# The first sparse tile's down rows summed by TensorE on four column groups, dense queries and ups in three passes

## The chip, the cores and the metric

One core of a Trainium2 chip. The metric is device time in microseconds of one execution: 2183.6 us before, the median of 3 runs (2182.3 to 2185.1).

## The reference

One layer over T = 640 tokens (512 of a prompt, 128 of eight streams), d = 1024: gated conv and retention branches, then a PEER layer, then a norm. The change touches PEER alone:

```python
q = (hb @ w_q)                       # 8 heads x 2 sides x 128
s = einsum(q, sub_keys)              # scores of 128 keys a side
# top 16 a side, top 16 of their sums: 16 experts e a head, weights g = softmax
a = gelu(einsum('thkd,td->thk', u_tab[e], hb))   # "ups": dot with row e of u
out = einsum('thk,thkd->td', g * a, v_tab[e])    # "downs": weighted sum of rows of v
```

There are 128 x 128 experts, and each token uses 128 of them. All is float32.

## The kernel before

Five tiles of 128 tokens. The first NS = 2 are **sparse**: for each of 256 "rows" r (a tile and one of its 128 picks), GpSimd gathers one row of u and one of v for each of the 128 tokens (128 x 1024, 512 KB each, one token in a partition). VectorE takes the dot with h (`dot`, L1446), ScalarE the gelu and the weight (`pair_gelu`), and VectorE adds weight times the v row to x (`pair_step`, L1463). Rows come in pairs, a pair's dots run two pairs ahead. The other three tiles (TD = 384 tokens) are **dense**: every up tile e of 128 experts is multiplied with h of all 384 tokens (`up`, L1833), gelu by ScalarE on the way out of PSUM (L950), stored to `acts` in DRAM; the gates (softmax weights, zero where an expert isn't picked) are built from one-hots by VectorE (`onehots`, L1483 and L1485: 48 blocks of 8 tokens) and TensorE (`scatter`, L1848), and stored as `gates`. Then 128 down tiles: VectorE forms p = acts x gates (`weigh`, L1500) and TensorE adds p times the v tile (`down_three`, L1890 to L1892).

A product in "three passes" splits both float32 operands into a high part (ScalarE's copy to F32R) and a low part (VectorE's difference) and sums high x high, high x low, low x high in single-pass F32R matmuls. Before, w_in, w_out and the downs (lows L1509 and L1515, highs L996 and L998) work so; queries (L1793) and ups are plain f32 matmuls.

Order: sparse queries (2 x 16 tiles of wq), dense queries (16 tiles), ups (128), downs (128). SP loads each tile of 512 KB to a ring of four (`plain_in`, L623) once the tile four before it has been used. VectorE runs retrieval (top 16, L1354 to L1428) for the five tiles, with pairs between its steps; then the 48 one-hot blocks with eight pairs; six pairs before the downs and 48 beside them (`pair_at`, `pair_after`). TensorE's scores and turns stand at fixed up tiles (SCORES_AT, PICKT_AT). GpSimd's gathers go through 14 slots in a fixed order (`rows_order`, L732), each waiting for the slot's last user.

## Time and profile before

| | |
|---|---|
| median of 3 runs | 2183.6 us |
| the profiled execution | 2185.9 us, its span 2184.1 |
| TensorE matmul busy | 98% of the span |
| VectorE / ScalarE / GpSimd busy | 80% / 28% / 39% |
| DMA | 732 MB, mean 335 GB/s |

A busy share counts an engine's instructions and not what the end waits for; the chain of waits goes back from the last instruction to what released it. In a list of single instructions the distance from start to start is the pace; the duration shown can overlap the next one's. An f32 matmul shows as two records, an F32R matmul as one.

### The profile page before, as it was taken

The page shows a single profiled execution, that of the slowest core. Times are in us where ns is not written, and L with a number is a line of the kernel's source. Part 1 is how long each engine was busy: PE and PEld are TensorE (multiplying, and loading weights), DVE is VectorE, ACT ScalarE, POOL GpSimd, SP SyncE. Part 2 cuts the span into 40 slices and gives each one's busy share as a digit, 9 for nine tenths or more (in the row PEclk, how much of TensorE's full clock was granted, in tenths as well). Part 3 has the DMA queues.
Part 4 walks back from the last instruction along what each step waited for, and adds up shares of the span by engine and source line. Part 5 has one row for each costly group of instructions (what it writes and reads, how often), then busy time and mean ns, then how long its engine had stood idle before and what let it go on. Part 6 is the DMA issues. An engine that isn't in the chain of part 4 may idle for free.

```text
span 2184.1 us, 31103 instructions
## 1 busy us (share of the span) xinstructions
PE 2139.8 (98%) x10569; PEld 1706.0 (78%) x10569; DVE 1746.6 (80%) x3270; ACT 619.3 (28%) x1197; POOL 860.8 (39%) x606
## 2 busy tenths in 40 slices
PE   6999999999999999999999999999999999999997
PEld 6999989999998985655565565677767888888886
DVE  2577586676765286898989979999969999999998
ACT  4212213132223111121211211233324444443434
POOL 4222122223333004475685675411145444444440
PEclk9999999999999999999999999999999999999999
DMA  5999999989983458999999999888999999999995
GB/s 191 300 329 308 300 299 330 333 299 326 305 287 136 137 195 336 336 372 412 397 410 412 383 412 412 299 290 298 301 340 411 414 414 413 414 414 414 414 415 202
DMA packets 312713, 732.28 MB, mean 335 GB/s; under 512 B 30208, under 2 KB 162048, under 8 KB 312576
## 3 DMA queue, kind: packets, MB, share of 16 engines
q1 hardware_dynamic: 188352, 436.52, 55.4%
q0 software_dynamic: 73728, 268.47, 31.3%
q10 hardware_dynamic: 50496, 25.59, 3.9%
q8 instruction: 70, 1.15, 0.2%
q14 instruction: 67, 0.55, 0.1%
HBM read 602.46 MB, written 128.00 MB: 334 GB/s over the span
## 4 chain that ended last, share of the span: by engine, by line
PE 61%; DMA 16%; DVE 14%; issue 4%; SPq 2%; ACT 1%; POOL 0%; DVEq 0%; ACTq 0%
PE ps L1833 29%; DMA b<-acts 12%; PE ps L1793 6%; PE ps L1596 6%; PE ps L1595 6%; PE ps L1594 6%; DMA b<-in_u_t 4%; PE ps L1848 4%; DVE b L1463 3%; DVE b L1509 2%; DVE b L1446 1%; DVE b L1515 1%; DVE b L1500 1%; SPq L527 1%; DVE b L1103 1%
## 5 line engine op out<-in xcount | busy, mean ns | idle before, releaser
L1833 PE MATMUL ps<-b,b 128*128 128x384 f32 x2048 | 665.6, 486 | 0.0
L732 POOL DMA_INDIRECT b<-u_rows,b x256 | 362.6, 1416 | 677.9 <-DVE b L1446 489.1
L1833 PEld LDWEIGHTS ps<-b,b 128*128 128x128 f32 x2048 | 386.8, 190 | 263.4
L695 POOL TENSOR_TENSOR b<-b,b 128x1024 fp32r<-128x1024 f32 x80 | 196.8, 2463 | 468.6 <-ACT b L745 464.0
L1463 DVE SCALAR_TENSOR_TENSOR b<-b,b,b 128x1024 f32<-128x1024 f32 x256 | 330.8, 1292 | 49.0 <-ACT b L966 32.6
L1594 PE MATMUL ps<-b,b 128*128 128x320 f32 x1152 | 364.5, 316 | 0.0
L1595 PE MATMUL ps<-b,b 128*128 128x320 f32 x1152 | 357.0, 310 | 0.0
L1596 PE MATMUL ps<-b,b 128*128 128x320 f32 x1152 | 357.0, 310 | 0.0
L732 POOL DMA_INDIRECT b<-in_peer_v,b x256 | 288.8, 1128 | 118.1 <-issue 76.9
L1446 DVE CUSTOM_DVE_ANT_0 b<-b,b 128x1024 f32<-128x1024 f32 x256 | 312.5, 1221 | 25.3 <-DMA b<-u_rows,b 23.8
L1103 DVE STREAM_TRANSPOSE b<-b 128x1024 f32<-128x1024 f32 x128 | 158.0, 1241 | 186.5 <-DMA b<-in_u_t 178.7
L1890 PE MATMUL ps<-b,b 128*128 128x512 f32 x768 | 299.5, 390 | 2.9 <-DVE b L1515 2.9
L1891 PE MATMUL ps<-b,b 128*128 128x512 f32 x768 | 299.9, 391 | 0.0
L1892 PE MATMUL ps<-b,b 128*128 128x512 f32 x768 | 298.7, 389 | 0.0
L1594 PEld LDWEIGHTS ps<-b,b 128*128 128x128 f32 x1152 | 217.6, 189 | 1.0
L1595 PEld LDWEIGHTS ps<-b,b 128*128 128x128 f32 x1152 | 217.4, 189 | 1.0
L1596 PEld LDWEIGHTS ps<-b,b 128*128 128x128 f32 x1152 | 217.2, 189 | 0.0
L950 ACT ACTIVATE b<-ps 128x384 f32<-128x384 f32 x128 | 62.6, 489 | 494.2 <-PE ps L1833 494.2
L1890 PEld LDWEIGHTS ps<-b,b 128*128 128x128 f32 x768 | 144.0, 188 | 35.9 <-issue 4.8
L1891 PEld LDWEIGHTS ps<-b,b 128*128 128x128 f32 x768 | 144.2, 188 | 30.1
L1892 PEld LDWEIGHTS ps<-b,b 128*128 128x128 f32 x768 | 144.2, 188 | 30.0
L1509 DVE TENSOR_TENSOR b<-b,b 128x1024 fp32r<-128x1024 f32 x128 | 155.8, 1217 | 12.3 <-ACT b L996 9.7
(164 smaller groups left out, 2414.0 us busy)
## 6 DMA issues: line engine op xcount, KB each, us to landing
b<-in_u_t SPq DMA_DIRECT2D x256, 512.0 KB, 6.5
u_rows<-b SPq DMA_DIRECT2D x512, 128.0 KB, 4.4
b<-in_peer_v SPq DMA_DIRECT2D x128, 512.0 KB, 22.1
b<-in_w_in SPq DMA_DIRECT2D x72, 512.0 KB, 6.4
b<-in_wq SPq DMA_DIRECT2D x48, 512.0 KB, 4.4
gates<-b ACTq DMA_DIRECT2D x12, 2048.0 KB, 8.3
b<-gates SPq DMA_DIRECT2D x32, 768.0 KB, 17.4
acts<-b SPq DMA_DIRECT2D x120, 192.0 KB, 7.9
```

The lines of the kernel that those rows point to most:

```text
L695: nc.gpsimd.tensor_tensor(lo[u][:, :], raw[:, u, :], hi[u][:, :].bitcast(F32), ALU.subtract).then_inc(lo_ready, 1)
L732: nc.gpsimd.indirect_dma_start(slots[n % SLOTS][:, :], None, u_rows if kind == "u" else v_rows, bass.IndirectOffsetOnAxis(ap=row_id[:, r_ ...
L1446: nc.vector.tensor_tensor_reduce(up_row, up_row, h_row[:, r_ // P, :], 1.0, 0.0, ALU.mult, ALU.add, dots[:, r_ // PAIR % LINES, r_ % PAIR: ...
L1463: nc.vector.scalar_tensor_tensor(token_rows, down_row, row_w[:, b % LINES, i:i + 1], token_rows, ALU.mult, ALU.add).then_inc(row_done, 1)
L1509: nc.vector.tensor_tensor(v_lo[n % HALVES][:, :], down_tile(e), v_hi[n % HALVES][:, :].bitcast(F32), ALU.subtract).then_inc(v_split, 1)
L1594: nc.tensor.matmul(out, wa_hi[u][:, cols], h_hi[:, k, tok], start=(k == 0), stop=False)
L1595: nc.tensor.matmul(out, wa_hi[u][:, cols], h_lo[:, k, tok], start=False, stop=False)
L1596: last = nc.tensor.matmul(out, wa_lo[u][:, cols], h_hi[:, k, tok], start=False, stop=(k == KT - 1))
L1833: last = nc.tensor.matmul(ps[:, up_bank(e), 0:TD], w[:, k * P:(k + 1) * P], h2[:, k, SD:T], start=(k == 0), stop=(k == KT - 1))
L1890: nc.tensor.matmul(out, p_hi[:, u, tok], v_hi[n][:, cols], start=(e == 0), stop=False)
L1891: nc.tensor.matmul(out, p_hi[:, u, tok], v_lo[n][:, cols], start=False, stop=False)
L1892: last = nc.tensor.matmul(out, p_lo[:, u, tok], v_hi[n][:, cols], start=False, stop=(e == NKEY - 1))
```

## The change

- `NPAIR` counts the second sparse tile's pairs only: 64, with 6 beside the one-hots, 4 before the downs (`NPAIR_U` = 10) and 54 beside the downs.
- First sparse tile: all 128 dots first (5 in each of the 9 gaps of the second retrieval, the others behind it). One gelu and one multiplication give all weights. Row numbers and weights are turned by TensorE, and GpSimd gathers the down rows per token ("t": the 128 v rows of one token, one in a partition), in the order of four quarters of 32 tokens. In each of 32 steps (`sum_rows`, behind one up tile each, m = 77 to 108) TensorE sums four tokens' rows: 4 tokens x 2 halves of 512 columns, f32, each with 32 columns of weights (a window that is zero but for the token's own column), to its quarter of the PSUM partitions. VectorE adds the result to x once.
- Dense queries and ups (N3 = 144 tiles, m = 0 to 143) in three passes: ScalarE makes the tile's high part (`up_tile_high`), VectorE the low part in place of the raw tile (`lows`), TensorE 24 F32R matmuls (`in_three`). The three high buffers lie in the memory of the sparse tokens' h.
- Where VectorE makes the lows, and where the one-hots' scatters, scores and turns stand on TensorE, is computed by a planner (`plan`).
- x of the dense tiles is stored to DRAM (`x_kept`) before the queries and read back in the downs, since the high part of dense h takes its memory. One v tile, not two, is loaded ahead of the downs.

```diff
-NPAIR = ROWS // PAIR
+NPAIR = P // PAIR
+N3 = 2 * PH + NKEY
+HIGHS = 3
+WINDOWS = 4
+SUM_GROUPS = 4
+NSUM = P // SUM_GROUPS
+DOTS_AT_FIRST = 4
+DOTS_INSIDE = 5
+DOTS_BEHIND_HOT = 7
+PAIRS_BESIDE_HOTS = 6
+BEFORE_DOWNS = 4
+LEAD = 3.0
...
+    def retrieval(tt, inside=()):
+        for i in range(INSIDE + 1):
+            yield ("retrieval", tt, i), 5.2
+            if 0 < i:
+                for step in inside:
+                    yield step()
+            if i in (2, 6):
+                yield ("inside", tt, i), 0.0
+        yield ("retrieved", tt), 0.0
+    dots = iter(range(P))
+    yield from retrieval(0)
+    for _ in range(DOTS_AT_FIRST):
+        yield ("dot", next(dots)), 1.25
+    yield from retrieval(1, [lambda: (("dot", next(dots)), 1.25)] * DOTS_INSIDE)
+    for r_ in dots:
+        yield ("dot", r_), 1.35
+    yield ("dots_done",), 3.0
+    for tt in range(NS, TT):
+        yield from retrieval(tt)
+    b = 0
+    yield ("picks_out",), 6.0
+    for blk_ in range(NHOT):
+        yield ("hot", blk_), 3.25
+        if blk_ == DOTS_BEHIND_HOT:
+            for r_ in range(AHEAD * PAIR):
+                yield ("dot", P + r_), 1.25
+        for _ in range(pairs_behind_hot(blk_)):
+            yield ("pair", b), 5.0
+            b += 1
+    for _ in range(BEFORE_DOWNS):
+        yield ("pair", b), 5.0
+        b += 1
+    yield ("end",), 0.0
...
+    lows, begins = {}, [812.0]
+    t, n, sums_at, hots_at = 772.0, 0, N3, N3
+    hots_end = 2 * PH + FIRST_DOWN
+    def hot_tile(blk_):
+        return hots_at + blk_ * (hots_end - hots_at) // NHOT
+    def begin(m):
+        while len(begins) <= m:
+            i = len(begins) - 1
+            us = 4.25 if i < 2 * PH else 4.4
+            if sums_at <= i < sums_at + NSUM:
+                us += 2.0
+            if hots_at <= i < hots_end:
+                us += 1.8 * sum(1 for b in range(NHOT) if hot_tile(b) == i)
+            begins.append(begins[-1] + us)
+        return begins[m]
+    for key, us in dve_steps():
+        if key == ("hot", 0):
+            hots_at = n + 1
+        if key[0] == "hot" and key[1] >= HOTS:
+            t = max(t, begin(hot_tile(key[1] - HOTS) + 1))
+        if key == ("dot", P):
+            t = max(t, begin(sums_at + NSUM) + 1.0)
+        while n < N3 and (begin(n) - LEAD <= t or key == ("end",)):
+            n += 1
+            t += 1.15
+        if key == ("retrieval", NS, 1):
+            sums_at = n + 1
+        lows[key] = n
+        t += us
+    return lows, sums_at, [hot_tile(b) - 2 * PH for b in range(NHOT)]
...
+def token_of(q):
+    return (q % SUM_GROUPS) * (P // SUM_GROUPS) + q // SUM_GROUPS
 def rows_order():
-    order = [("u", r) for r in range(AHEAD * PAIR)]
-    for r in range(ROWS):
+    order = [("u", r) for r in range(P)]
+    order += [("t", q) for q in range(P)]
+    order += [("u", P + r) for r in range(AHEAD * PAIR)]
+    for r in range(P, ROWS):
...
+        raw_lo = at(x_from + TT * D * 4, [P, GROUP, D], F32R)
+        u_hi = [at(o_, [P, D], F32R) for o_ in (h_from + 36864, h_from, h_from + 4096)]
...
+                if i == 2 * GROUP - 1:
+                    for tt in range(NS, TT):
+                        sp.wait_ge(xs_ready, TT + tt + 1)
+                        sp.dma_start(x_kept[tt - NS, :, :], x[:, tt, :]).then_inc(x_stored, 16)
...
+            for i in range(ND):
+                sp.dma_start(x[:, NS + i, :], x_kept[i, :, :]).then_inc(x_back[i], 16)
...
+                if (kind, r_) == ("t", 0):
+                    pool.wait_ge(idT_ready, 1)
...
+            def dense_high(i):
+                if i == 0:
+                    act.wait_ge(x_stored, 16 * ND)
+                tok = slice(i * P, (i + 1) * P)
+                act.wait_ge(h_ready, 2 * TT + 2 * (NS + i) + 2)
+                nc.scalar.activation(hd_hi[:, :, tok], h2d[:, :, tok], ACT.Copy).then_inc(hd_high, 1)
+            def up_tile_high(m):
+                i = 2 * A_WQ + m
+                act.wait_ge(loaded[i % GROUP], 16 * ((N_WQ + i) // GROUP + 1))
+                act.wait_ge(a_used, A_MIX + (2 * A_WQ if m < HIGHS else i - HIGHS + 1))
+                nc.scalar.activation(u_hi[m % HIGHS][:, :], raw[:, i % GROUP, :], ACT.Copy).then_inc(up_high, 1)
...
+            def window(j):
+                if j == 0:
+                    act.wait_ge(wT_ready, 1)
+                    act.wait_ge(zeros_ready, 1)
+                if j >= WINDOWS:
+                    act.wait_ge(rows_summed, j - WINDOWS + 1)
+                src = wT_a[:, :].rearrange("p (c j) -> p c j", c=SUM_GROUPS)[:, :, j:j + 1]
+                nc.scalar.activation(windows[:, j % WINDOWS, :, 31:32], src, ACT.Copy).then_inc(window_ready, 1)
...
+            def lows(*key):
+                while low_next[0] < LOWS[key]:
+                    m = low_next[0]
+                    at_ = (2 * A_WQ + m) % GROUP
+                    dve.wait_ge(up_high, m + 1)
+                    nc.vector.tensor_tensor(raw_lo[:, at_, :], raw[:, at_, :], u_hi[m % HIGHS][:, :].bitcast(F32),
+                                            ALU.subtract).then_inc(up_low, 1)
+                    low_next[0] += 1
+            def dense_low(i):
+                tok = slice(i * P, (i + 1) * P)
+                dve.wait_ge(hd_high, i + 1)
+                nc.vector.tensor_tensor(hd_lo[:, :, tok], h2d[:, :, tok], hd_hi[:, :, tok].bitcast(F32),
+                                        ALU.subtract).then_inc(hd_ready, 1)
...
-            retrieval(0)
-            for r_ in range(AHEAD * PAIR):
-                dot(r_)
-            for tt in range(1, TT):
-                retrieval(tt, next_pair)
-                for i in range(GAP if tt < TT - 1 else 0):
-                    next_pair()
-                    if i == 1 and tt >= NS:
-                        picks_out(tt)
-            assert taken[0] == NPAIR_R
...
+                def between():
+                    seen[0] += 1
+                    lows("retrieval", tt, seen[0])
+                    if tt == 1:
+                        if seen[0] == 2:
+                            row_numbers_out()
+                        for _ in range(DOTS_INSIDE):
+                            next_dot()
+                    if tt == NS and seen[0] == 1:
+                        row_weights_out()
+                    if tt == TT - 1 and seen[0] >= 8:
+                        picks_out(seen[0] - 8 + NS)
+                return between
...
+            lows("retrieval", 0, 0)
+            retrieval(0, inside(0))
+            lows("retrieved", 0)
+            for _ in range(DOTS_AT_FIRST):
+                next_dot()
+            lows("retrieval", 1, 0)
+            retrieval(1, inside(1))
+            lows("retrieved", 1)
+            while at_dot[0] < P:
+                next_dot()
+            lows("dots_done")
+            row_weights()
+            for tt in range(NS, TT):
+                lows("retrieval", tt, 0)
+                retrieval(tt, inside(tt))
+                lows("retrieved", tt)
+            lows("picks_out")
             picks_out(TT - 1)
-            for blk_ in range(TD // BLK):
+            for blk_ in range(NHOT):
+                lows("hot", blk_)
+                if HOT_AT[blk_] == UP_IN_TWO - 4 and HOT_AT[blk_ - 1] < UP_IN_TWO - 4:
+                    row_sums_out()
                 onehots(blk_)
-                if blk_ % 6 == 4:
+                if blk_ == DOTS_BEHIND_HOT:
+                    for r_ in range(P, P + AHEAD * PAIR):
+                        lows("dot", r_)
+                        dot(r_)
+                for _ in range(pairs_behind_hot(blk_)):
                     next_pair()
             for i in range(BEFORE_DOWNS):
-                if i == WEIGH_BEFORE:
-                    down_inputs(0)
                 next_pair()
+            lows("end")
...
+            def in_three(m, out):
+                pe.wait_ge(up_low, m + 1)
+                hi, lo = u_hi[m % HIGHS][:, :], raw_lo[:, (2 * A_WQ + m) % GROUP, :]
+                for k in range(KT):
+                    cols = slice(k * P, (k + 1) * P)
+                    nc.tensor.matmul(out, hi[:, cols], hd_hi[:, k, :], start=(k == 0), stop=False)
+                    nc.tensor.matmul(out, hi[:, cols], hd_lo[:, k, :], start=False, stop=False)
+                    last = nc.tensor.matmul(out, lo[:, cols], hd_hi[:, k, :], start=False, stop=(k == KT - 1))
+                last.then_inc(a_used, 1)
+            def dense_query(m):
+                i = 2 * A_WQ + m
+                pe.wait_ge(evac, A_MIX + i - 1)
+                in_three(m, ps[:, 2 + i % UP_BANKS, 0:TD])
...
+            def sum_rows(j):
+                pe.wait_ge(window_ready, j + 1)
+                places = [PLACE["t", j * SUM_GROUPS + c] for c in range(SUM_GROUPS)]
+                for n in places:
+                    pe.wait_ge(row_in[n % SLOTS], 16 * (n // SLOTS + 1))
+                for dh in range(2):
+                    for c, n in enumerate(places):
+                        last = nc.tensor.matmul(ps[32 * c:32 * c + 32, 2 + dh, :],
+                                                windows[:, j % WINDOWS, c, 31 - j:63 - j],
+                                                slots[n % SLOTS][:, dh * 512:(dh + 1) * 512],
+                                                start=(j == 0), stop=(j == NSUM - 1))
+                last.then_inc(rows_summed, 1)
...
+            for m in range(N3):
+                if m < A_WQ:
+                    dense_query(m)
+                else:
+                    up(m - A_WQ)
...
+                if 0 <= m - SUMS_AT < NSUM:
+                    sum_rows(m - SUMS_AT)
+                for blk_ in range(NHOT):
+                    if HOT_AT[blk_] == m - A_WQ:
```

## Rows read from the trace of the kernel before

**Rows 1.** The page's 40 slices: TensorE's clock, and what DMA moved.

```profile
PEclk9999999999999999999999999999999999999999
...
GB/s 191 300 329 308 300 299 330 333 299 326 305 287 136 137 195 336 336 372 412 397 410 412 383 412 412 299 290 298 301 340 411 414 414 413 414 414 414 414 415 202
```

**Rows 2.** Stretches: us, busy PE PEld DVE ACT POOL, PEclk, DMA share, GB/s.

```profile
886.00:1392.00 506.00, 506.00 (x1637) 302.66 (x1636) 462.71 (x1107) 95.11 (x294) 321.99 (x250) 1.00 1.01 394
...
1392.00:1604.00 212.00, 211.12 (x1157) 159.25 (x1156) 203.52 (x496) 73.43 (x150) 39.99 (x35) 1.00 0.88 289
...
1646.00:2155.00 509.00, 507.59 (x2232) 418.37 (x2231) 483.50 (x656) 215.02 (x396) 233.20 (x178) 1.00 1.01 408
```

**Rows 3.** The chain of work, pieces merged: start, us, what.

```profile
797.89 7.21 PE ps L1793 x32
...
1268.98 123.84 PE ps L1833 x384
...
1600.80 3.57 PE ps L1848 x32
...
1604.37 36.14 PE ps L1833 x112
...
1831.21 20.82 DMA b<-acts
```

**Rows 4.** The down matmuls of L1890: durations, first and last start.

```profile
L1890 PE MATMUL ps<-b,b x768: 387/389/689, 1645.2 to 2172.6; 128*128 128x512 f32 x192
```

**Rows 5.** TensorE in order of time: w_in products, downs.

```profile
559.70 0.31 PE L1595 MATMUL ps<-b,b 128*128 128x320 f32 x1
...
569.53 0.31 PE L1596 MATMUL ps<-b,b 128*128 128x320 f32 x1
...
1789.70 0.39 PE L1892 MATMUL ps<-b,b 128*128 128x512 f32 x1
...
1801.98 0.39 PE L1892 MATMUL ps<-b,b 128*128 128x512 f32 x1
```

**Rows 6.** VectorE in order of time: the first retrieval, the first dot.

```profile
769.52 0.30 DVE L1354 MAX8 b<-ps 128x8 f32<-128x128 f32 x1 [24.13 <-PE ps L1819]
...
817.07 0.29 DVE L1428 SCALAR_TENSOR_TENSOR b<-b 128x128 uint32<-128x128 f32 x1
...
822.39 1.23 DVE L1446 CUSTOM_DVE_ANT_0 b<-b,b 128x1024 f32<-128x1024 f32 x1 [5.03 <-DMA b<-u_rows,b]
```

**Rows 7.** Groups by line: operands, count, busy us, mean ns, idle before.

```profile
L1833 PE MATMUL ps<-b,b 128*128 128x384 f32 x2048 | 665.6, 486 | 0.0
...
L996 ACT ACTIVATE b<-b 128x1024 fp32r<-128x1024 f32 x128 | 134.1, 1048 | 14.9 <-PE ps L1892 14.9
```

**Rows 8.** VectorE in the downs: a low, a pair, the next tile.

```profile
1657.78 1.21 DVE L1509 TENSOR_TENSOR b<-b,b 128x1024 fp32r<-128x1024 f32 x1
...
1658.92 0.54 DVE L1515 TENSOR_TENSOR b<-b,b 128x384 fp32r<-128x384 f32 x1
...
1663.69 1.22 DVE L1446 CUSTOM_DVE_ANT_0 b<-b,b 128x1024 f32<-128x1024 f32 x1
...
1668.41 0.55 DVE L1500 TENSOR_TENSOR b<-b,b 128x384 f32<-128x384 f32 x1
```

**Rows 9.** VectorE: the first of two one-hot blocks.

```profile
1394.38 2.14 DVE L1483 TENSOR_SCALAR b<-b,b,b 128x128 f32<-128x128 f32 x8
...
1397.69 2.13 DVE L1483 TENSOR_SCALAR b<-b,b,b 128x128 f32<-128x128 f32 x8
```

**Rows 10.** DMA in 1646 to 2155 us: total; acts loads, median us to landing.

```profile
DMA packets 52709, 207.88 MB, mean 408 GB/s; under 512 B 5873, under 2 KB 5873, under 8 KB 52675
...
b<-acts SPq DMA_DIRECT2D x30, 768.0 KB, 20.1
```

**Rows 11.** Loads of up tiles (L623), 1101 to 1388 us.

```profile
DMA to landing us min/median/max: 5.1/6.7/8.5
```

**Rows 12.** VectorE's waits in 1646 to 2155 us: us, times, longest.

```profile
DVE b L1500 <- DMA b<-acts: 22.9, 12, 2.6
```

321 lines of the change are left out of this document (203 added, 118 removed).

## Prediction

> **What bounds the kernel now.** I read the slices of the page first, then busy time by stage, then the chain of work, then single instructions. The slices [rows 1] say that TensorE is busy nearly throughout, at full clock, and that the DMA engines move 412 to 415 GB/s in many slices, which is the most they reach anywhere. The table by stage [rows 2] shows two stages behind 810 us. From 810 to 1646 us (dense queries, ups, scatters) TensorE has no idle time, VectorE is 91 to 96% busy beside the ups and the scatters, and DMA is near its top. From 1646 to 2155 us (downs) three things are close together: TensorE without a gap, VectorE 483.5 of 509 us, DMA 408 GB/s. The chain [rows 3] walks along TensorE alone in the first: 24 up tiles in 123.84 us, so **5.16 us a tile**, a scatter of two blocks 3.57, so **1.785 us** a block (and 3.57 for the scores of a tile, which are as many matmuls of the same shape), ups over at 1640.5. The first down matmul is at 1645.2 [rows 4]. In the downs the chain goes through VectorE's rows and the acts load (20.8 us), so it is no longer plainly TensorE: whatever loads VectorE or DMA more will lengthen it.
>
> **Dense queries and ups in three passes.** An up tile is now 8 f32 matmuls, recorded as 16 of 0.3225 us; the change makes them 24 of one pass. Their price is read where the kernel already does this: 320 columns, 67 steps from 559.70 to 569.53, 0.1467 us each; 512 columns, 54 steps in 12.28 us, 0.2274 [rows 5]. Over columns/2.4 GHz that is 13.4 and 14.1 ns, so 384 columns take 0.174 us, a tile 4.17, with hand-over **4.2 us**; bounds 4.16 and 4.32 (w_out's 512-column pitch of 0.233 adds 20 ns). The gain is 144 x 0.96 = 138 us.
>
> Its start is later: the high parts lie in the memory of the sparse tokens' h, so they wait for the last sparse query. That one ends at 797.89 + 7.21 - 5.16 = 799.9 [rows 3]. The lows of tiles 0 and 1 stand in VectorE's order before the last tenth of the first retrieval, which runs 769.5 to 817.4 (47.9 us [rows 6]), at about 809.5. So the first dense tile starts at **811** instead of 799.9: 11 us lost.
>
> The added halves: 144 highs on ScalarE at 1.05 us [rows 7], which is 28% busy, so nothing. 144 lows on VectorE at **1.15 us** of its time (the same low in the downs: 1657.78 to the next start at 1658.92 [rows 8]), 166 us. The queries' three dense halves (3 x 1.2 us) and the stores of x_kept fall into VectorE's wait of 24 us before 769.5 [rows 6]; the three ScalarE copies that feed them stand before the sparse queries' evacuations and may hold TensorE back by 2 us there, if two PSUM banks don't cover 3.2 us. On SP the stores of x_kept stand before sparse query tile 8's load; what they wait for (the scaled rows) is done by then, so nothing. If that cover failed, the tile loads behind it would come late by as much.
>
> **The first sparse tile's down rows.** 128 adds leave VectorE. But 140 leave this stage, as only 20 of the second tile's rows are now done before the downs instead of 160 rows of both; and 152 dots instead of 164. At 1.20 and 1.15 us a row ([rows 8]: a pair with dots is 1663.69 to 1668.41, 4.72 us) that is -168 - 14 + 166 = **-16 us** for VectorE before the downs. TensorE gets 32 steps of 8 matmuls, 16 records of 512 columns, 0.3225 x 512/384 = 0.43 us each. No row has column groups. Bounds: all four groups side by side, 4 x 0.43 = 1.7 us a step; none, 16 x 0.43 = 6.9. I take **2.2**, near the lower end, because the four groups write disjoint quarters of the partitions and in the nearest rows [rows 5] a matmul follows the last at 14 ns over its columns, so its weights load beside running work.
>
> The Trainium skill ("TensorE: Matmul & The Clock Gate", part 3) has three column tiles of 32 at 2.38 times the speed of one after another; carried to four that would be an estimate of 2.2 us, and no run here shows it yet.
>
> **The stage as a sum.** TensorE from 811: 144 x 4.2 = 604.8; scores of four tiles 4 x 3.57 = 14.3; turns 3; sums 32 x 2.2 = 70.4; scatters 48 x 1.785 = 85.7; together 778, so 1589. VectorE from 769.5: five retrievals 239.5; 132 dots x 1.26 = 166; lows 166; 48 one-hot blocks x 3.31 [rows 9] = 159; ten pairs 47; gathers' first landing 7 [rows 6]; small steps 8: together 792, so 1562. Both fit, but they are tied: each low stands at a fixed place of VectorE's order and its tile can't start before it. So phase by phase, with the places that the planner's arithmetic gives (74 lows before the dots end, 105 before the picks, 136 before the sixth pair, 144 at the end). POOL, which issues the gathers, now waits once for the turned row numbers before the down rows; behind it nothing but those rows is queued, and they come ready near 860, long before dot 128. ScalarE's new waits (a window for the sums, three steps ahead) stand before evacuations that have two banks of cover. Up to tile 74: TensorE 311 + 7 = 318 (1129), VectorE 769.5 + 96 + 161 + 85 + 8 = 1119; TensorE leads. Tiles 74 to 105: TensorE 206 (1335), VectorE 144 + 36; TensorE. One-hots: VectorE 159 + 5 + 28 + 35 = **227**, TensorE 218; VectorE leads, begin 1332, so 1562 with some stalls. Last eight tiles 34: **1596**. With the same 4.7 us to the first down it stands at **1600**, 45 us earlier than 1645.2.
>
> DMA in this stage: from 823 (row numbers) to 1119 the dots' 128 rows, 74 tiles and 58 stored acts are 67 + 39 + 11 = 117 MB, 283 us at 0.414 MB/us: it fits barely. In the sums each step wants 4 x 0.524 + 0.721 = 2.82 MB, 6.8 us against 6.4, made up by 14 rows fetched ahead: no cost taken, 10 us as the bound.
>
> **The downs.** 108 adds and 104 dots are left instead of 96 and 92, six pairs more: 6 x 4.72 = 28 us of VectorE. Bytes: 24 rows x 0.524 + 1.57 (x read back) = 14.1 MB on 207.9 [rows 10]; 222/0.4145 = 536 us for what took 509, +27. VectorE: 483.5 + 28.3 + its waits of 25.5 = 537, +28. Two resources are then full together, which costs a little: **+30 us**, bounds +20 (the waits shrink as the work fills them) and +45 (the acts load, 20.1 us now [rows 10], stretches and is waited for more than the 22.9 us of today [rows 12]). TensorE's 128 x 4.1 hides in it. So of the 138 us that the passes give, 70 go to the sums, 11 to the start, some 9 to the one-hots, and 30 to the downs.
>
> Net: -45 + 30 = -15 us. The profiled execution took 2185.9 (span 2184.1) and stands 2.3 above the median; 2183.6 - 15 gives **2168**. Later rows (final norm) are unchanged.
>
> **Rivals.** (a) *Staircase* (the one that ends slower). An f32 matmul is two records for the same column group (x2048 records for 1024 in the code [rows 7]). If matmuls start strictly in order, a group's second record waits for its first, and only the second of one group overlaps the first of the next: 9 slots of 0.43 = 3.87 us a step instead of 2.2. VectorE has no slack to lose there, TensorE leads: 32 x 1.67 = +53, **2221**. It decides from 2.7 us a step (15/32 above 2.2). For it: the records are strictly in line today. Against: nothing in the trace.
> The same section of the Trainium skill says that matmuls keep program order in start and end; that would be this rival's condition, and by it the time would be the 2221 of the sentence before; no run here shows it.
>
> (b) *No groups at all*: 6.9 us a step, +150, **2318**.
> (c) *The ring of four tiles is too short.* A tile is loaded when the one four before it is done, so three tiles (12.6 us) must hold the load, the high (1.05) and VectorE's lead of about 3 us: 8.4 us are left for the load. It takes 6.7 us today, at most 8.5, at a full DMA [rows 11], but with 140 GB/s wanted by this queue, and 172 then. At 9.5 us a tile costs (9.5 + 4.15)/3 = 4.55; 60 tiles x 0.35 = +21, and the sums' 10 us: 2189 to **2199**.
> (d) *The downs stay at TensorE's pace*, +5 instead of +30: **2143**. Against it speak the flat 412 to 415 GB/s.
>
> **How the numbers follow.** Forecast 0.68, with 2150 to 2188 from 4.16 to 4.32 us a tile, 1.7 us a step and +20 to +45; (a) 0.13; (b) 0.04; (c) 0.10; (d) 0.05. 2142 to 2212 holds nearly all of the first, (c) and (d): 0.8. A measurement of this kernel can tell about 0.2% (4.4 us) from no change. Faster: 0.61 of the forecast and (d): 0.66. Within: the forecast's edge and (c)'s: 0.08. Slower: (a), (b), most of (c), the rest: 0.26.
>
> **What would show it.** First dense matmul at 811; 4.2 us a tile up to tile 77; 6.4 us a tile in the sums, with matmuls of the four groups starting together; ups over near 1596; VectorE without waits only in the one-hots; downs 4.3 us a tile at 412 GB/s or more, with waits for the acts or rows. Wrong if the sums' step is over 2.7 us, if VectorE waits for ScalarE's highs in the dots' phase, or if the downs keep 4.1 us a tile.

## The result and the profile after

The changed kernel is slower: **2224.5 us** (median of 4 runs, 2220.0 to 2225.9) against 2183.4 (4 runs, 2182.3 to 2185.1), a ratio of 1.0184, 95% interval 1.0166 to 1.0202. The profiled execution took 2225.9 us, with a span of 2224.1. The stages after it, answering to [rows 2]; columns as there:

```profile
886.00:1155.00 269.00, 255.87 (x1460) 252.91 (x1458) 233.84 (x413) 95.92 (x125) 180.06 (x114) 0.99 0.97 367
1155.00:1390.00 235.00, 208.61 (x1308) 159.87 (x1309) 181.97 (x700) 60.45 (x106) 125.77 (x112) 0.95 0.95 365
1390.00:1652.00 262.00, 252.41 (x1725) 245.91 (x1724) 246.55 (x526) 116.20 (x201) 79.92 (x60) 0.99 0.92 315
1652.00:2200.00 548.00, 521.32 (x2252) 423.23 (x2251) 516.32 (x694) 219.57 (x417) 257.06 (x199) 0.99 1.00 405
```

Where TensorE was practically never idle between 810 us and the downs, it now has gaps in the dots' phase, in the sums and beside the one-hots, its granted clock is below 1.00 there, and yet VectorE isn't full either: 234 of 269, 182 of 235, 247 of 262 us. No engine fills its stage; that is the sign of two engines that wait for each other. Who waits for whom, TensorE between 810 and 1652 us and then VectorE between 769 and 1652 (us, times, longest):

```profile
PE ps L2080 <- DVE b L1635: 59.1, 15, 12.5
PE ps L2149 <- DMA b<-in_peer_v,b: 4.9, 7, 1.7
...
DVE b L1635 <- ACT b L1148: 48.0, 32, 3.8
DVE b L1624 <- PE ps L2126: 26.3, 2, 15.7
DVE b L1679 <- DMA b<-u_rows,b: 16.3, 19, 4.4
DVE b L1660 <- PE ps L2120: 9.7, 1, 9.7
DVE b L1535 <- issue: 5.0, 1, 5.0
```

TensorE (first matmul of a tile, L2080) waited 59 us for lows (L1635). VectorE waited 48 us for highs (L1148). A high waits for its tile's load, and it stands in ScalarE's order behind the eviction of the tile three before, which waits for TensorE. VectorE also waited 26 us for the turned picks and 10 us for the turned weights of the first sparse tile, which TensorE turns after fixed tiles; 16 us for gathered rows. One such meeting in order of time, tile 74 (start, us, engine, line; ScalarE, VectorE, TensorE):

```profile
1152.87 1.06 ACT L1148 ACTIVATE b<-b 128x1024 fp32r<-128x1024 f32 x1 [1.90 <-DMA b<-in_u_t]
...
1148.54 1.22 DVE L1635 TENSOR_TENSOR b<-b,b 128x1024 fp32r<-128x1024 f32 x1
1150.99 0.31 DVE L1655 TENSOR_TENSOR b<-b,b 128x128 f32<-128x128 f32 x1 [1.23 <-ACT b L1153]
1151.44 3.04 DVE L1535 MAX8 b<-ps 128x8 f32<-128x128 f32 x15
...
1158.90 2.36 DVE L1635 TENSOR_TENSOR b<-b,b 128x1024 fp32r<-128x1024 f32 x2
...
1154.06 0.34 PE L2082 MATMUL ps<-b,b 128*128 128x384 f32 x1
1160.27 0.66 PE L2080 MATMUL ps<-b,b 128*128 128x384 f32 x1 [5.87 <-DVE b L1635]
1160.72 0.52 PE L2081 MATMUL ps<-b,b 128*128 128x384 f32 x1
1161.04 0.52 PE L2082 MATMUL ps<-b,b 128*128 128x384 f32 x1
```

The high of tile 74 was ready at 1153.9, TensorE was done with tile 73 at 1154.2, but the low's place is behind a whole round of the third retrieval, and came at 1158.9. Behind the gap TensorE restarts at the lower of its two clock levels (1.2 GHz, a granted clock of 0.50), 0.32 us a matmul instead of 0.173:

```profile
1160.50:1164.50 4.00, 4.00 (x13) 4.00 (x14) 0.76 (x1) 0.00 (x0) 0.00 (x0) 0.50 1.03 410
```

Up to the first down there are eight such stretches (at 810.6, 848, 874, 971, 1161, 1181, 1369 and 1643 us) with 88 steps of 0.32 us, each behind a gap of TensorE of 3.1 to 12.5 us; over the pitch of 0.1733 these cost 13 us.

The matmuls and a step of the sums, which come out close to the forecast (a tile takes 4.16 us in the median between tiles 20 and 72, and 6.24 with a step of the sums behind it):

```profile
1249.71 0.34 PE L2082 MATMUL ps<-b,b 128*128 128x384 f32 x1
1249.89 0.34 PE L2080 MATMUL ps<-b,b 128*128 128x384 f32 x1
1250.06 0.34 PE L2081 MATMUL ps<-b,b 128*128 128x384 f32 x1
1250.23 0.34 PE L2082 MATMUL ps<-b,b 128*128 128x384 f32 x1
1250.50 1.92 PE L2149 MATMUL ps<-b,b 128*32 128x512 f32 x16
1252.36 0.44 PE L2080 MATMUL ps<-b,b 128*128 128x384 f32 x1
```

Below, "tile n" is the start of the first matmul of dense tile n (the 8n-th record of L2080 behind the first). Forecast and measured: tile 0 at 811 and 810.2; tile 74 at 1129 and **1160.3**; tile 106 at 1335 and **1389.6**; tile 136 at 1562 and **1611.8**; first down at 1600 and **1652.7** (before: 1645.2 [rows 4]). From there to the end of the span 571.4 us, where it was 538.9 before.

### The profile page after: what moved, and what is told of

Read it like the earlier page. It is cut to its first block, busy times and chain, and to the rows that moved or that the text cites. A ratio compares the mean times of both kernels' runs of the same rounds, so it can differ in the third digit from the quotient of the medians.

```text
span 2224.1 us, 34471 instructions
## 1 busy us (share of the span) xinstructions
PE 2090.8 (94%) x12235; PEld 1896.4 (85%) x12235; DVE 1762.4 (79%) x3290; ACT 732.6 (33%) x1185; POOL 883.5 (40%) x606
## 4 chain that ended last, share of the span: by engine, by line
PE 37%; DMA 25%; DVE 22%; issue 7%; POOL 6%; ACT 2%; SPq 2%; DVEq 0%; ACTq 0%
DMA b<-in_peer_v,b 14%; POOL b L868 6%; PE ps L1871 5%; PE ps L1872 5%; PE ps L1873 5%; DMA b<-in_u_t 5%; PE ps L2080 4%; PE ps L2081 4%; PE ps L2082 4%; DVE b L1716 3%; DVE b L1696 2%; PE ps L2149 2%; DVE b L1679 2%; DMA b<-acts 2%; DVE b L1718 2%
## 5 line engine op out<-in xcount | busy, mean ns | idle before, releaser
L868 POOL DMA_INDIRECT b<-u_rows,b x256 | 381.0, 1488 | 634.6 <-DVE b L1679 428.3
L2080 PE MATMUL ps<-b,b 128*128 128x384 f32 x1152 | 399.4, 347 | 61.6 <-DVE b L1635 59.1
L2081 PE MATMUL ps<-b,b 128*128 128x384 f32 x1152 | 391.6, 340 | 0.0
L2082 PE MATMUL ps<-b,b 128*128 128x384 f32 x1152 | 391.5, 340 | 0.0
L868 POOL DMA_INDIRECT b<-in_peer_v,b x256 | 295.1, 1153 | 180.2 <-PE ps L2149 86.1
L2080 PEld LDWEIGHTS ps<-b,b 128*128 128x128 f32 x1152 | 221.6, 192 | 91.0 <-issue 88.5
L1635 DVE TENSOR_TENSOR b<-b,b 128x1024 fp32r<-128x1024 f32 x144 | 175.3, 1223 | 49.4 <-ACT b L1148 48.0
```

The source lines that it names most:

```text
L868: nc.gpsimd.indirect_dma_start(slots[n % SLOTS][:, :], None, u_rows if kind == "u" else v_rows, bass.IndirectOffsetOnAxis(ap=number, axis= ...
L2080: nc.tensor.matmul(out, hi[:, cols], hd_hi[:, k, :], start=(k == 0), stop=False)
L2081: nc.tensor.matmul(out, hi[:, cols], hd_lo[:, k, :], start=False, stop=False)
L2082: last = nc.tensor.matmul(out, lo[:, cols], hd_hi[:, k, :], start=False, stop=(k == KT - 1))
```

## The experiments

Three theories on why the ups end 50 us late were set against each other: **L**, the gathers fill DMA, so tile loads, highs and lows come late; **O**, the fixed order makes the two engines stand on each other; **VectorE full**, 144 lows don't fit whatever the order. The single runs were timed beside the kernel before on the same chip, which took between 2184 and 2190 us there; differences below about 6 us between single runs are not settled by them.

**1. Thinned gathers in the dots** (114 of the first sparse tile's 128 gathers of up rows fetch 32 rows instead of 128, so most of each of these dots is left out):

```diff
+                some = 32 if kind == "u" and SLOTS <= n < P else P
                 nc.gpsimd.indirect_dma_start(
-                    slots[n % SLOTS][:, :], None, u_rows if kind == "u" else v_rows,
-                    bass.IndirectOffsetOnAxis(ap=number, axis=0),
+                    slots[n % SLOTS][0:some, :], None, u_rows if kind == "u" else v_rows,
+                    bass.IndirectOffsetOnAxis(ap=number[0:some, :], axis=0),
```

> The changed kernel, but 114 of the first sparse tile's 128 up-row gathers fetch 32 rows instead of 128 (so the first tile's output isn't the reference's): some 45 MB less on DMA up to tile 74, the same instructions on every engine. Theory L (the gathers fill DMA, tile loads land at 8.8 us instead of 6.7, ScalarE's highs and then VectorE's lows come late): the loads fall to 5 us or so, VectorE's 32 us of waits for highs before 1152 go, the third retrieval starts near 1120 instead of 1151, and the whole takes 25 to 35 us less, about 2193. Theory O (the fixed order: each engine waits for a step that the other has behind its own wait): the loads get faster, the stage keeps most of its idle time, under 10 us less, 2215 or more.

Measured: 2208.8 (before 2189.3). DMA between 979 and 1115 us fell from 394 to 251 GB/s, tile 74 came at 1142.0 instead of 1160.3, the first down at 1635.7. The tile loads between 979 and 1115 us took 5.0 us in the median instead of 8.8, and yet VectorE still waited 29.4 us for highs before 1150, where it had waited 32.4. So the gathers have a share of some 18 us by tile 74. It is not DMA's for certain: a gather of 32 rows also takes GpSimd less time to issue: the 135 and 133 issues that began between 830 and 1150 us took GpSimd 204 us in the changed kernel and 163 here. No run changed one of the two without the other. L alone, which asked for 25 to 35 us of the time and for these waits to go, fails; so does O alone, which asked for 2215 or more.

**2. Turns earlier** (all is computed):

```diff
-PICKS_AFTER = {tt: LOWS["retrieval", TT - 1, 8] - 1 for tt in range(NS, TT - 1)}
+PICKS_AFTER = {tt: LOWS["retrieval", TT - 1, 4] + 1 for tt in range(NS, TT - 1)}
...
-WEIGHTS_AFTER = LOWS["retrieval", NS, 1] - 1
+WEIGHTS_AFTER = LOWS["dots_done",] - 1
```

> The changed kernel with TensorE's turns placed earlier: the first tile's weights behind tile 73 instead of 75, the picks of the first two dense tiles behind tile 100 instead of 102; nothing else. VectorE waited 9.7 us for the one and 15.7 + 10.6 us for the others, TensorE stood idle 9 us and 7.5 us beside them. Theory O: each engine's wait there shrinks by the two tiles, and some 10 to 20 us come off, 2205 to 2214. Theory L: the phase's pace is set by loads and bytes, the time moves by under 5 us.

Measured: 2208.9. The wait for the weights is gone, that for the picks 19.2; tile 77 at 1172.7 (was 1186.7), first down at 1635.3. Two constants of the order give back 17 us at the first down, with no work taken from VectorE: O is real, and a full VectorE alone doesn't explain the loss.

**3. More dots inside the second retrieval.**

```diff
-DOTS_INSIDE = 5
+DOTS_INSIDE = 8
```

> The changed kernel with 8 instead of 5 dots in each of the second retrieval's nine gaps; 52 instead of 79 stand behind it, and the planner moves the lows with them. The same bytes, spread over more time. Theory L: fewer loads fall into the stretch in which DMA is full, 8 to 15 us less (2210 to 2216). Theory O: no clear sign, within 6 us either way, since the order is as tight as before.

Measured: 2220.7, tile 74 at 1157.3, first down at 1650.3: within 6 us, as O said; spreading the dots another way changes nothing.

**4. No lows** (the low parts of the dense tiles are left out; the third pass takes the high part again, so TensorE's work is the same):

```diff
-                    dve.wait_ge(up_high, m + 1)
-                    nc.vector.tensor_tensor(raw_lo[:, at_, :], raw[:, at_, :], u_hi[m % HIGHS][:, :].bitcast(F32),
-                                            ALU.subtract).then_inc(up_low, 1)
...
-                pe.wait_ge(up_low, m + 1)
-                hi, lo = u_hi[m % HIGHS][:, :], raw_lo[:, (2 * A_WQ + m) % GROUP, :]
+                pe.wait_ge(up_high, m + 1)
+                hi = lo = u_hi[m % HIGHS][:, :]
```

> The changed kernel without the lows of the 144 tiles (TensorE uses the high part a third time, the same number of matmuls; the low part's share of the queries and ups is left out). VectorE loses 166 us of work and TensorE no longer waits for VectorE at each tile. Theory O and a too full VectorE both say that ups then end near 1590 (TensorE's own sum of 772 us from about 803) and the whole near 2165. Theory L alone (tile loads too late for TensorE itself) says that the ring of four still holds TensorE back: 2190 or more, with TensorE waiting for ScalarE's highs.

Measured: **2150.7**, clock 0.993. Its stages and TensorE's waits from 800 to 1577 us:

```profile
886.00:1119.00 233.00, 232.55 (x1323) 227.76 (x1322) 140.89 (x250) 88.38 (x114) 119.12 (x100) 1.00 1.02 407
1119.00:1329.00 210.00, 202.10 (x1307) 153.65 (x1307) 149.86 (x677) 59.55 (x104) 122.10 (x115) 1.00 0.98 381
...
PE ps L2146 <- DMA b<-in_peer_v,b: 6.7, 11, 1.2
```

TensorE runs from tile 0 at 796.2 to tile 74 at 1115.5, that is 319.3 us where the forecast had 318, with tile loads that take 10.0 us in the median (8.8 in the changed kernel) and DMA at 407 GB/s. So neither a full DMA nor the ring of four tiles holds TensorE when no low stands between load and matmul. Downs from 1577.5: the lows, with the waits they make and a start that is 14 us later, cost the ups 75 us. This refutes L alone; O and a full VectorE both foretold it (near 1590 and 2165), so it doesn't tell these two apart.

**5. Lows later** (on top of 2): the plan that writes the order places each low 1 us before its tile instead of 3, and, in the second kernel, also reckons 4.6 us a dense tile.

```diff
-LEAD = 3.0
+LEAD = 1.0
...
-            us = 4.25 if i < 2 * PH else 4.4
+            us = 4.6
```

> The early turns of the run before (time 2208.9), and the written order now puts each low 1 us before its planned tile instead of 3, so VectorE comes to the lows later and its dots, retrievals and one-hots earlier. Theory O (the two engines stand on each other at fixed places of a fixed order, because TensorE runs some 10 to 20 us behind the plan's times from tile 32 on, so the highs that a low reads are not there): VectorE's waits for highs fall from 48 us to under 30, and the time falls by another 5 to 12 us, to 2197 to 2204. Rival S (the low is on TensorE's path with no slack; later lows are taken from TensorE one for one): the waits only change their engine, the time stays at 2206 to 2214.

> As the run beside it, and the plan behind the written order is told 4.6 us a dense tile instead of 4.25 and 4.4, which is what tiles took in the changed kernel up to tile 74 with its stalls (350 us by 74 tiles is 4.73). The lows come later still against VectorE's other work. Theory O: the order is now made for the times that occur, VectorE waits for highs under 20 us, third retrieval begins before 1145, time 2185 to 2200. Rival S: TensorE starves for lows in the dots instead, tile 74 is not earlier than 1158, time 2206 or more.

Measured: 2215.5 and 2225.6 (before 2188.0): 7 and 17 us slower than the early turns. With the first, VectorE's waits for highs didn't fall at all (55.3 us over the whole stage, 47.1 with the early turns). With the second VectorE waits 19 instead of 33 us for highs before 1155, but TensorE's waits for lows rise from 44.2 (14 times) to 58.8 us (25 times). My wish to fit the plan to the measured times was wrong, and the gain that O had promised didn't come. The rival, a low has no slack and what VectorE saves there TensorE loses, is the nearer one, though the first time lies just above its 2206 to 2214.

**6. The tile buffers untied** (on top of 2). A low is written over its tile; here it goes into a ring of its own, paid with gather slots, so the tile's buffer takes the next load as soon as the low is computed. The second kernel has two tiles for lows and 12 slots, the third three tiles and 11 slots, with lows placed 5 us before their tiles and the last picks turned one tile earlier.

```diff
-SLOTS = 14
+SLOTS = 11
+LOW_RING = 3
...
-                else:
-                    sp.wait_ge(a_used, A_MIX + i - 3)
+                elif i < 2 * A_WQ + GROUP:
+                    sp.wait_ge(a_used, A_MIX + i - 3)
+                else:
+                    sp.wait_ge(up_low, i - 2 * A_WQ - 3)
...
+                    if m >= LOW_RING:
+                        dve.wait_ge(a_used, A_MIX + 2 * A_WQ + m - LOW_RING + 1)
-                    nc.vector.tensor_tensor(raw_lo[:, at_, :], raw[:, at_, :], u_hi[m % HIGHS][:, :].bitcast(F32),
+                    nc.vector.tensor_tensor(own_lo[m % LOW_RING][:, :], raw[:, at_, :], u_hi[m % HIGHS][:, :].bitcast(F32),
```

> The early turns, and the lows of the dense tiles go into a ring of three tiles of their own (taken from the gather ring, 14 slots down to 11) instead of over the tile itself, so that a tile's buffer is free, and its successor's load starts, as soon as its low is computed, some 15 us before TensorE is done with it. Theory R (the tile buffers tie the engines: a load starts when TensorE ends the tile four before, lands 6.7 to 8.8 us later, the high and the low then come at the last moment, so VectorE waits for highs): VectorE's waits for highs fall from 48 us to under 15, tile 74 starts before 1145, time 2180 to 2197. Rival H (what ties them is the ring of three highs and the place of the high in ScalarE's order, behind the eviction of tile m-3): the waits stay above 30 us, the time at 2204 to 2212. Rival G (eleven slots are too few, VectorE waits for gathered rows instead): over 2212.

> As the run beside it with two tiles for the lows and 12 slots for the gathers. Theory R: as there, but a low must wait for TensorE's end of the tile two before, so within 5 us of it either way. Rival G: it is faster than the three-tile version by as much as VectorE waits less for gathered rows. Rival H: 2204 to 2212 here too.

> As the three-tile ring, with each low written 5 us ahead of its planned tile instead of 3 and the last picks turned one tile earlier. With the buffers untied VectorE can run ahead; the lead then covers TensorE's jitter, theory R: 0 to 8 us faster than the three-tile ring at 3 us, and VectorE's wait for the picks falls from 19 us to under 14. Rival H: highs are not there five microseconds ahead (they need the end of the tile three before, 8 us ahead at best), VectorE waits more, over 5 us slower than beside it.

Measured: 2205.9, 2222.0 and 2208.5 (before 2190.0). With three tiles VectorE's wait for highs before 1155 us halves (32.9 to 15.9) and tile 74 comes at 1150.2 instead of 1158.3; but its waits for gathered rows rise from 13.5 to 33.2 us with eleven slots, one of 7.8 us just before the downs, which start at 1634.8 as before. With two tiles the low waits for TensorE (63.7 us in 37 waits): the same meeting in a new place, and 13 us slower than with 14 slots and no own ring. With the longer lead tile 74 comes at 1144.1 and the first down at 1629.9, but the downs take 576.8 us instead of 569.2, and in the time nothing is gained beyond a single run's doubt. The theory behind this experiment (the tile buffers tie the engines: highs' waits under 15 us, tile 74 before 1145, time 2180 to 2197) failed. Its rival H had said that the ring of three highs, and the high's place in ScalarE's order behind an eviction, would keep the waits for highs above 30 us and the time at 2204 to 2212: over the whole stage they are 32.9 us (47.1 before), and the time is 2205.9.

The three-tile version again, in three rounds:

> The best version that keeps the whole computation, timed in three rounds against the kernel before: early turns, and the lows in a ring of their own. From one run, 2205.9 against 2190.0, it is 0.7 per cent slower than before. If its gain of 19 us over the changed kernel is real, the ratio is 1.007 to 1.011; if it was chance of the one run, 1.013 or more.

Measured: **2207.4** (2205.8 to 2212.0), ratio to before 1.0112, interval 1.0096 to 1.0129. That lies at the edge of what a real gain had been said to give (1.007 to 1.011). It keeps the whole computation and mends 18 of the changed kernel's 41 us, but doesn't reach the kernel before; nor did any other version that keeps the computation. It stands 23 us above the kernel before, the early turns alone 20 us in one run, so that the ring of lows adds anything to them in the whole time is not shown.

**7. Both causes taken away at once** (6 with three tiles, and the thinned gathers of 1, so the dots leave most of their sum out):

```diff
+                some = 32 if kind == "u" and SLOTS <= n < P else P
```

> Early turns, lows in a ring of three tiles of their own with 11 gather slots, and the gathers of the first sparse tile's up rows fetch 32 of 128 rows (its dots then leave most of the sum out). The two causes up to tile 74 taken together: thinned gathers alone brought tile 74 from 1160 to 1142, the own ring alone from 1158 to 1150. If they are separate causes (late loads for want of DMA; late loads for want of a free buffer) they add: tile 74 at 1132 to 1138, VectorE's waits for highs under 10 us and for rows under 5 us in the dots, time 2186 to 2196. If both only shorten the same wait, or VectorE's own program is what is left: tile 74 at 1140 to 1146, time 2197 to 2204.

Measured: 2195.6; tile 74 at 1139.4, first down at 1625.0. The chain of work up to tile 74, of this kernel and then of the changed one:

```profile
by line: PE ps L2086 27.2%; PE ps L2087 27.0%; PE ps L2088 26.7%; DVE b L1641 2.9%; DVE b L1685 2.8%; DVE b L1543 2.5%; PE ps L2116 2.1%; DVE b L1539 1.8%; DVE b L1549 1.4%; issue 1.0%; ACT b L1152 0.9%; DVE b L1548 0.8%; DVE b L1603 0.7%; 
...
by line: POOL b L868 29.5%; PE ps L2080 10.8%; PE ps L2081 10.6%; PE ps L2082 10.6%; DMA b<-u_rows,b 6.7%; issue 6.4%; DMA b<-in_u_t 4.0%; DMA b<-in_wq 4.0%; DVE b L1635 3.2%; DVE b L1679 2.7%; DVE b L1539 2.4%; PE ps L2110 2.0%; DVE b L153
```

In the changed kernel TensorE's three passes are 32% of the chain and the gathers' issue on GpSimd (L868) 30%; with both causes gone TensorE is 81% of it. What the issue alone costs is not shown, since the thinned gathers also shortened it (experiment 1). Behind the ring the thinned gathers give 11 us (1150.2 to 1139.4), but by themselves they had given 18 (1160.3 to 1142.0), and the ring by itself 8. Together that would be 26; both make 19. So the two in part shorten the same wait. The likely one is the high's for its tile's load: 85 us between 830 and 1150 us in the changed kernel (94 with the early turns), 29 with the thinned gathers, 38 with the ring, 3 with both. The expectation's signs are split: the time lies in the range of separate causes, tile 74 between the two ranges, and VectorE's waits for highs didn't fall under 10 us. ScalarE's highs waiting for loads between 830 and 1150 us, in the changed kernel and in this one, then this one's waits of VectorE up to 1140 us and of TensorE from 808 to 1140:

```profile
ACT b L1148 <- DMA b<-in_u_t: 85.0, 50, 2.9
...
ACT b L1152 <- DMA b<-in_u_t: 2.8, 3, 2.0
...
DVE b L1641 <- ACT b L1152: 24.2, 26, 3.5
...
PE ps L2086 <- DVE b L1641: 22.6, 5, 12.3
```

Late loads are gone as a cause here, and VectorE waits for highs all the same. What is left in front of a high is its place behind the eviction of the tile three before, which waits for TensorE: the rival H of experiment 6. That was not tested by an edit of its own. Such a wait of VectorE costs time only where TensorE then waits for the low: beyond the start of 12.3 us that was 10.3 us in four waits, the longest, 5.7 us, again before tile 74, whose low stands behind a round of the third retrieval.

**8. Lows on GpSimd** (on top of 2: those of tiles 113 to 135, beside the one-hots, where GpSimd is idle for 180 of 262 us; in the second kernel 11 instead of 6 pairs of rows are done there too):

```diff
+G0, G1 = 113, 136
...
+            def pool_lows(to):
+                while pool_next[0] < min(to, G1):
+                    m = pool_next[0]
+                    at_ = (2 * A_WQ + m) % GROUP
+                    pool.wait_ge(up_high, m + 1)
+                    pool.wait_ge(up_low, m)
+                    nc.gpsimd.tensor_tensor(raw_lo[:, at_, :], raw[:, at_, :], u_hi[m % HIGHS][:, :].bitcast(F32),
+                                            ALU.subtract).then_inc(up_low, 1)
+                    pool_next[0] += 1
...
-PAIRS_BESIDE_HOTS = 6
+PAIRS_BESIDE_HOTS = 11
```

> The early turns, and the lows of the dense tiles 113 to 135 (beside the one-hots) are GpSimd's, which is idle there between its gathers (2.44 us each by its own subtractions of the earlier stage, against 1.22 on VectorE). It tells apart whether VectorE's filled program sets the end of the ups. Theory V (VectorE is full in the one-hot stage: 251 of 267 us): 23 x 1.22 = 28 us go from VectorE, of which TensorE (scatters and tiles, plan 1558 at tile 136) gives 20 to 28: downs from 1607 to 1615, time 2180 to 2190. Rival B (the two engines slow each other while both run two-input operations, as the gathers' 1.98 against 0.94 us hint): VectorE's one-hots and pairs grow by as much as is saved, time 2203 to 2212. Rival D (a ScalarE or load wait takes over): lows late on GpSimd, TensorE waits for it, time over 2212.

> As the run beside it, and 11 instead of 6 of the pairs of gathered rows beside the one-hots, which take VectorE's 28 us again (5 x 4.7 = 24) and move 5 x 4 gathers, 10.5 MB, out of the downs, where DMA is full (408 GB/s: 26 us), into the one-hot stage (312 GB/s there). Theory D of the thinned gathers (DMA sets the downs): the downs fall from 571 to 548 to 555, the ups end as early as with the early turns alone (1628 to 1638), time 2180 to 2190, no better than beside it but by the other way. If VectorE rather than DMA sets the downs, the same pairs come off VectorE too, and the sum is the same; if neither does, the time is 2205 to 2215.

Measured: 2235.0, ratio 1.0221 (1.0186 to 1.0256), and 2229.8, ratio 1.0197 (1.0161 to 1.0234). Rival B, and harder than it said: 2.2% over before instead of the 0.9% of the early turns. The time would also fit rival D, a low that comes late on GpSimd, but TensorE waited for no low of GpSimd; it waited 22.2 us for VectorE's one-hots (3.0 with the early turns alone). The one-hots' groups between 1440 and 1590 us with the lows on VectorE, then between 1440 and 1620 with the lows on GpSimd; below, single pieces of the latter (VectorE, then GpSimd):

```profile
L1716 DVE TENSOR_SCALAR b<-b,b 128x128 f32<-128x128 f32 x256 | 69.0, 344 | 1.3
...
L1745 DVE TENSOR_SCALAR b<-b,b 128x128 f32<-128x128 f32 x263 | 110.5, 495 | 3.1
...
1486.32 2.14 DVE L1745 TENSOR_SCALAR b<-b,b 128x128 f32<-128x128 f32 x8
1489.70 4.02 DVE L1745 TENSOR_SCALAR b<-b,b 128x128 f32<-128x128 f32 x8
1494.97 4.22 DVE L1745 TENSOR_SCALAR b<-b,b 128x128 f32<-128x128 f32 x8
1500.43 2.14 DVE L1745 TENSOR_SCALAR b<-b,b 128x128 f32<-128x128 f32 x8
...
1488.33 3.51 POOL L853 TENSOR_TENSOR b<-b,b 128x1024 fp32r<-128x1024 f32 x1 [6.98 <-ACT b L1173]
1495.67 2.40 POOL L853 TENSOR_TENSOR b<-b,b 128x1024 fp32r<-128x1024 f32 x1 [3.83 <-ACT b L1173]
```

Eight one-hots take 2.14 us, and 4.0 to 4.2 when a low of GpSimd runs beside them: VectorE stands still for about 2 us of the low's 2.4. The other way round, the low that began beside a product of VectorE (1488.33) took 3.51 us instead of 2.40. The Trainium skill ("SBUF — State Buffer", the section on its two separate sides) states that the two engines share one port pair, and that a VectorE operation in a 2-port mode, or with two inputs in SBUF beside a GpSimd operation that reads SBUF, and the GpSimd operation take it as an exclusive lock for a whole instruction; these rows agree. So a VectorE low of 1.2 us was traded for some 2 us in which VectorE stood still.

The second kernel says something on the downs all the same: they last 545.6 us (1681.3 to 2226.9) instead of 571.4, with DMA still at 414 GB/s.

**9. Thinned gathers in the downs** (the gathers of later rows, from the 24th of the second sparse tile on, fetch 32 of 128 rows each):

```diff
+                some = 32 if r_ >= P + 24 else P
```

> Leaves out three quarters of the bytes of the gathers of the rows from the 24th of the later tiles on (each fetches 32 of its 128 rows; the sparse tiles' values are then wrong), all instructions stay. It cuts the DMA in the downs from 408 GB/s to some 200. Theory D (the ten microseconds and more by which the downs are longer than TensorE's and VectorE's busy time come of DMA: gathers of 31 to 34 us on the chain): downs from first matmul to the end of the span fall from 571 us to 540 to 550, the time from 2224 to 2195 to 2205. Rival V (VectorE's pairs, 507 of 535 us busy, and TensorE's 511 set the downs, whatever DMA does): the downs stay within 5 us of 571, the time over 2215.

Measured: 2200.8, up to the downs as the changed kernel (tile 136 at 1612.2, first down 1654.9), and from there 544.1 us. Its downs, as a stage:

```profile
1655.00:2190.00 535.00, 527.53 (x2305) 430.85 (x2303) 525.12 (x722) 225.42 (x430) 233.15 (x198) 1.00 0.82 266
```

With all instructions kept and DMA at 266 GB/s, 27 of the 32.5 us by which the downs grew are gone; TensorE and VectorE are now both over 525 of 535 us busy. The downs' loss is DMA's.

**10. One part of the change alone**: the sums on column groups, but dense queries and ups as plain f32 products (the highs and lows of the tiles and of h are left out as well).

```diff
-                pe.wait_ge(up_low, m + 1)
-                hi, lo = u_hi[m % HIGHS][:, :], raw_lo[:, (2 * A_WQ + m) % GROUP, :]
+                w = plain_tile(2 * A_WQ + m)
                 for k in range(KT):
...
+                    last = nc.tensor.matmul(out, w[:, k * P:(k + 1) * P], h2d[:, k, :], start=(k == 0), stop=(k == KT - 1))
```

> One part of the change alone: the first sparse tile's down rows still go through TensorE on four column groups, but dense queries and ups are single f32 products as before the change (5.16 us a tile, no highs and lows), in the changed kernel's order. By the prediction's sum: 144 tiles x 5.16 from 800 is 1543, with 31 steps x 2.1 and the scatters, rows turned and banks as now 1650 to 1665; the downs then take 571: 2225 to 2240, so the three passes, with their 144 lows on VectorE and their stalls, win nothing against it at all. If the stalls come of VectorE's 144 lows, the plain ups run without any, at the pitch of 5.16 and 3.9 us a scatter step. The other way (the three passes pay in spite of the stalls, since the plain ups wait for VectorE just the same): over 2255.

Measured: 2274.4, the first down at 1707 us, no stall of TensorE. The stage, with the first two downs:

```profile
800.00:1716.00 916.00, 915.56 (x3751) 555.24 (x3750) 576.25 (x1679) 155.37 (x329) 369.38 (x315) 1.00 0.88 321
```

TensorE is busy without a gap, VectorE 576 of 916 us. The expectation of 1650 to 1665 for the first down was a slip of addition: from 800, 144 x 5.16 = 743, sums 66, scatters 86, scores and turns 17 make 1712, and 1707 was measured. So the other case holds: the three passes do pay, some 50 us (2274.4 in one run to 2224.5) of the 127 they could (138 less 11 for the later start), and the rest is lost where TensorE meets VectorE. The sums by themselves stand 86 us over the kernel before (2188.0): of the change's two parts, this is the one that loses.

## Why the prediction was wrong

**Right: every price of an instruction.** First dense tile at 810.2 for 811. Three passes at 0.1733 us a matmul, 4.16 us a tile (0.174 and 4.2). A tile with a step of the sums takes 6.24 us (6.4), so the step costs 2.08 (2.2): 16 records of 512 columns in 1.92 us, side by side on four column groups. That refutes rival (a), whose 2221 lies near the measured time by accident: its mechanism asked for 3.87 us a step. Rival (b) falls with it. The estimate of 2.2 us carried over from the Trainium skill's three column tiles ("TensorE: Matmul & The Clock Gate", part 3) agrees with the trace; its sentence that matmuls keep program order doesn't slow the groups here. TensorE's own work to tile 74 was 318 us and, left alone (experiment 4), took 319.3. The downs: +32.5 for +30, DMA limited by experiment 9 as the byte count said; rival (d) is out.

**Wrong: the step "Both fit, but they are tied".** I saw the tie, and then priced each phase at the larger of two engines' sums: tile 74 at max(1129, 1119), tile 106 at max(1335, ...), and so on. With only 10 us between the two sums up to tile 74, every wait of the one becomes a wait of the other, and I costed them at nothing. Measured against the forecast, the first down is 53 us late: 31 up to tile 74, 23 more to tile 106, 5 fewer to tile 136 (222 us for 227), and 3 on the last eight. TensorE waited 59 us for lows, 12.5 of them the start that the forecast had, and its stretches at the lower clock cost 13 more, a term the sum didn't have. Up to tile 74 this closes: TensorE took 350 us for work of 319, 25 of them waits behind the start and some 7 the lower clock. The starts of the first down show the parts: 1652.7 as changed, 1635 with the turns moved (17 us), 1625 with the buffers untied and the gathers thinned as well, 1577.5 without lows; the forecast was 1600. By tile 74, 19 us go with both the ring and the thinned gathers, of which late loads are the likely common part. Some 10 of the 31 are left with both gone: there TensorE waits 10 us for lows and loses 3 at the lower clock, and starts 3 earlier. The rounds of the third retrieval in front of tile 74's low make 5.7 of these; what the place of the high in ScalarE's order costs was not tested.

**Half right: rival (c)**, and the sentence on DMA in the dots' phase, that "it fits barely", which got no term in the sum. The condition, a load of 9.5 us, was met by some loads (up to 10.1 us) but not by the median (8.8 between 979 and 1115 us, at 415 to 417 GB/s from 1020 us on), and with a median of 10.0 us and no lows TensorE didn't wait. But with the low on the way the gathers, by their bytes or their issue, cost up to 18 us by tile 74. Load, high and low stand in one line, and I had costed each against its own limit. The text did name "if VectorE waits for ScalarE's highs in the dots' phase" as what would make it wrong; it is the 48 us row, 32 of them in that phase.

**Where the gain went.** In the forecast's terms 138 us by the passes; 70 to the sums, 11 to the start, 9 to the one-hots, 30 to the downs; and 53 more to meetings, clock and the gathers. The range's upper end, 2212, was set by (c) alone; a case in which VectorE and TensorE wait for each other at several per cent of a stage of 789 us was not in it.

## What to carry to other kernels

When two engines are both over 90% full and handed to each other tile by tile in a written order, the stage is not the longer of the two sums; here it was 7% longer (53 of 789 us), and TensorE's eight longest gaps each cost again at the lower clock. Ask of each per-tile hand-over how long the chain load, high, low, matmul is against its buffers, and what long piece of other work stands in front of it. Before moving work to an idle GpSimd, ask whether VectorE's work beside it needs the port that they share.

## What the runs showed of the hardware

- Four column groups of 32 run side by side also for f32 matmuls, each of which is two records: 16 records of 512 columns in 1.92 us.
- GpSimd's issue of a gather takes 0.94 us, and often up to 1.98 beside VectorE's back-to-back dots and lows, which read two tensors: of the 75 issues that began during a dot in the changed kernel 72 took over 1.1 us (median 1.88), of the 58 that began with VectorE idle none. Here in order of time, the last two beside VectorE's idle and its maxima of 1150 to 1154 us:

```profile
1143.76 1.40 POOL L868 DMA_INDIRECT b<-in_peer_v,b  x1 [0.30 <-issue]
1145.46 1.98 POOL L868 DMA_INDIRECT b<-in_peer_v,b  x1 [0.30 <-issue]
1147.74 1.69 POOL L868 DMA_INDIRECT b<-in_peer_v,b  x1 [0.30 <-issue]
1149.73 0.94 POOL L868 DMA_INDIRECT b<-in_peer_v,b  x1 [0.30 <-issue]
1150.98 0.94 POOL L868 DMA_INDIRECT b<-in_peer_v,b  x1 [0.30 <-issue]
```

- A GpSimd subtraction of 128x1024 (2.4 us) beside eight one-hots of VectorE stretches them from 2.14 to 4.0 to 4.2 us, as in experiment 8: one of the two stands still.
- TensorE's eight gaps of 3.1 to 12.5 us up to the first down were each followed by a stretch of 7 to 17 matmuls of 384 columns at 0.32 us instead of 0.173, at a granted clock of 0.50.
